# Feed-forward contraction of a hybrid decoder layer: accumulator set-up and the first half's layer norm move from GpSimd and ScalarE to VectorE

## The reference

```python
x = layer_norm(alpha * x + mix, ln1_g, ln1_b)
ff = jnp.square(jax.nn.relu(x @ w_ff1)) @ w_ff2
x = layer_norm(alpha * x + ff, ln2_g, ln2_b)        # alpha = 2 ** 0.25
```

## Time and profile before

| | us |
|---|---|
| median of 3 runs | 2074.1 |
| the three runs | 2073.32, 2074.1, 2076.65 |
| span of the profiled execution | 2073.1 |
| PE busy in it | 2050.5 (99%) |
| DVE, ACT, POOL busy | 1395.7, 993.8, 488.9 |
| bytes moved | 374.34 MB, mean 181 GB/s |

### The profile page before, as it was taken

How to read it: one execution, slowest core, us unless ns; L and a number is a source line. 1 busy time by engine, 2 the same in 40 slices (tenths; PEclk the granted TensorE clock), 3 DMA queues, 4 the chain that set the end, 5 groups by cost and what they waited for, 6 DMA issues and landing times. The chain is left out here.

```text
span 2073.1 us, 28942 instructions
## 1 busy us (share of the span) xinstructions
PE 2050.5 (99%) x11360; PEld 1678.8 (81%) x11360; DVE 1395.7 (67%) x1969; ACT 993.8 (48%) x1339; POOL 488.9 (24%) x537
## 2 busy tenths in 40 slices
PE   9999999999999999999999999999999999999998
PEld 8778788878887888788888888888788888778887
DVE  6687568656856698766657767566485645965477
ACT  5444544454444457655556545455333333633333
POOL 3000000000000013244301344345696600810000
PEclk9999999999999999999999999999999999999999
DMA  6144252425142524466666777868968555666664
GB/s 186 53 121 120 64 170 56 133 61 173 52 123 64 181 72 153 154 211 211 215 214 203 279 259 248 279 244 293 335 206 292 194 195 190 223 225 194 194 220 163
DMA packets 244327, 374.34 MB, mean 181 GB/s; under 512 B 18032, under 2 KB 119504, under 8 KB 244192
## 3 DMA queue, kind: packets, MB, share of 16 engines
q1 hardware_dynamic: 213536, 275.82, 41.2%
q0 software_dynamic: 30656, 96.67, 14.3%
HBM read 272.81 MB, written 99.61 MB: 180 GB/s over the span
## 5 line engine op out<-in xcount | busy, mean ns | idle before, releaser
L1751 DVE TENSOR_TENSOR w_lo<-w_b,w_hi 128x1024 fp32r<-128x1024 f32 x142 | 207.3, 1464 | 202.3 <-ACT w_hi L1718 202.3
L1751 DVE TENSOR_TENSOR w_lo<-raw,w_hi 128x1024 fp32r<-128x1024 f32 x142 | 198.9, 1405 | 119.0 <-ACT w_hi L1718 118.7
L1718 ACT ACTIVATE w_hi<-raw 128x1024 fp32r<-128x1024 f32 x142 | 150.2, 1059 | 217.8 <-PE main L71 86.9
L1718 ACT ACTIVATE w_hi<-w_b 128x1024 fp32r<-128x1024 f32 x142 | 150.0, 1057 | 173.9 <-PE aux L71 73.3
L69 PE MATMUL main<-xT_lo,w_hi 128*128 128x512 f32 x512 | 210.5, 411 | 0.0
L71 PE MATMUL main<-xT_hi,w_hi 128*128 128x512 f32 x512 | 200.1, 391 | 0.0
L70 PE MATMUL main<-xT_hi,w_lo 128*128 128x512 f32 x512 | 199.7, 390 | 0.0
L1130 DVE TENSOR_TENSOR w_lo<-raw,w_hi 128x1024 fp32r<-128x1024 f32 x114 | 138.8, 1222 | 89.1 <-ACT w_hi L805 87.4
L69 PE MATMUL sc<-x_lo,w_hi 128*128 128x512 f32 x448 | 174.4, 389 | 1.8 <-DVE z L2214 1.8
L70 PE MATMUL sc<-x_hi,w_lo 128*128 128x512 f32 x448 | 174.3, 389 | 0.0
L71 PE MATMUL sc<-x_hi,w_hi 128*128 128x512 f32 x448 | 174.3, 389 | 0.0
(11 more groups left out here) (305 smaller groups left out, 4667.7 us busy)
## 6 DMA issues: line engine op xcount, KB each, us to landing
raw<-in_w_in_dram SPq DMA_DIRECT2D x80, 512.0 KB, 3.8
h_dram<-z SPq DMA_DIRECT2D x64, 512.0 KB, 4.3
raw<-h_dram SPq DMA_DIRECT2D x112, 256.0 KB, 2.7
w_b<-h_dram SPq DMA_DIRECT2D x112, 256.0 KB, 2.7
h_dram<-h_s SPq DMA_DIRECT2D x48, 512.0 KB, 3.8
raw<-in_w_out_dram SPq DMA_DIRECT2D x32, 512.0 KB, 3.7
raw<-in_w_ff_dram SPq DMA_DIRECT2D x32, 512.0 KB, 6.4
w_b<-in_w_ff_dram SPq DMA_DIRECT2D x32, 512.0 KB, 4.7
```

Of the source, the lines that this page charges most:

```text
L1718: act.activation(hi, slot_tile(ff, m), ACT.Copy).then_inc(ff.hi_done, 1)
L1751: dve.tensor_tensor(lo, slot_tile(ff, m), hi.bitcast(F32), ALU.subtract).then_inc(ff.lo_done, 1)
```

## The change

Six things change, all in `feed_forward`.

- POOL loads the rows g1 and b1 and all accumulator tiles, and does no arithmetic on them. The scaling of the two rows is gone.
- DVE sets up the accumulators: `residual_scaled` is (acc * alpha) * g1 and `residual_shifted` is b1 * alpha + acc, both on 128x512. They stand around `slot_low` in slots k = 4, 6, 8, 10 of eight products (`INIT_PLACES`).
- The first half's statistics are split: column half 1 of tiles 0 to 7 in (0, 5) and (0, 6), column half 0 and the join at `FIRST_DONE`, which are slots 1, 4, 7, 10 of the last product of half 0 and of the first product of half 1.
- DVE finishes the first half with `centred` and `scaled` in the two slots after each join, as it does the second half's.
- ACT gives rstd only; its 128x1 copy and the 128x1024 normalisation of the first half are gone.
- POOL only stores the first half's tiles, when `out_ready` says so.

```diff
+FIRST_DONE = [(0, 6, 1), (0, 6, 4), (0, 6, 7), (0, 6, 10), (1, 0, 1), (1, 0, 4), (1, 0, 7), (1, 0, 10)]
+INIT_PLACES = [(0, 0), (0, 1), (0, 2), (0, 3), (0, 4), (0, 5), (1, 1), (1, 2)]
...
         load_row(g1_row, ln1_g)
         load_row(b1_row, ln1_b)
-        for c in range(4):
+        for c in range(NT):
             load_acc(0, c, 4 + 2 * c)
-        pool.wait_ge(row_landed, 16 * 2)
-        for row in (g1_row, b1_row):
-            pool.tensor_scalar(row[:, :], row[:, :], ALPHA, None, ALU.mult).then_inc(row_scaled, 1)
...
-        init(0)
         for c in range(NT):
             load_acc(1, c, 2 * KF + 2 * c)
         load_row(g2_row, ln2_g)
         load_row(b2_row, ln2_b)
-        init(1)
-        pool.wait_ge(row_landed, 16 * 4)
         for c in range(NT):
-            finish(c)
+            pool.wait_ge(out_ready, 2 * c + 2)
+            pool.dma_start(out_rows[P * c:P * c + P, :], acc[0][:, c, :]).then_inc(out_stored[c], 16)
...
+        def residual_scaled(hf, i):
+            c, d = INIT_ORDER[i]
+            cols = slice(512 * d, 512 * d + 512)
+            dve.wait_ge(row_landed, 16 * 2)
+            dve.wait_ge(acc_landed[hf][c], 16)
+            dve.scalar_tensor_tensor(out=acc[hf][:, c, cols], in0=acc[hf][:, c, cols], scalar=ALPHA,
+                                     in1=g1_row[:, cols], op0=ALU.mult, op1=ALU.mult).then_inc(init_step, 1)
...
+            init = None
+            if (hf, at) in INIT_PLACES and 4 <= k < 12 and k % 2 == 0:
+                init = divmod(4 * INIT_PLACES.index((hf, at)) + (k - 4) // 2, 16)
+                residual_scaled(*init)
             if s + 4 < 2 * CONTRACT_SLOTS:
                 slot_low(dve, ff, EXPAND_SLOTS + s + 4)
-            if hf == 1 and at == 0 and 2 <= k < 10:
-                statistics(0, k - 2, 28)
+            if init is not None:
+                residual_shifted(*init)
...
+            if (hf, at, k) in FIRST_DONE:
+                c = FIRST_DONE.index((hf, at, k))
+                half_statistics(0, c, 0, 24 if c < 4 else 28)
+                join_statistics(c)
+            elif (hf, at, k - 1) in FIRST_DONE:
+                if (hf, k) == (0, 2):
+                    dve.wait_ge(row_landed, 16 * 4)
+                centred(0, FIRST_DONE.index((hf, at, k - 1)), scale_step)
+            elif (hf, at, k - 2) in FIRST_DONE:
+                c = FIRST_DONE.index((hf, at, k - 2))
+                scaled(0, c, scale_step, c + 1, out_ready)
```

More of the change, by code:

```diff
@@ L2179, in _ @@
                 slot_high(act, ff, EXPAND_SLOTS + s + 4)
-            if hf == 1 and at == 0 and 3 <= k < 11:
-                normalise(0, k - 3)
+            if (hf, at, k) in FIRST_DONE:
+                inverse_deviation(0, FIRST_DONE.index((hf, at, k)))
             if hf == 1 and (at, k) in HEAD:
-                inverse_deviation(HEAD.index((at, k)))
+                inverse_deviation(1, HEAD.index((at, k)))
         for c in range(TAIL, NT):
-            inverse_deviation(c)
+            inverse_deviation(1, c)
     @block.vector
@@ L2203, in join_statistics @@
             dve.tensor_scalar(nmean[:, c:c + 1], mvar[:, c, 0:1], -1.0, None, ALU.mult).then_inc(ln_stats, 1)
[L2205 to L2208, removed]
         def completed(chunk, i, src, tile):
@@ L2298, in _, with centred, scaled, residual_shifted @@
         last_sum(CHUNKS - 1)
-        def centred(c, step):
-            dve.wait_ge(ln_stats, NT + c + 1)
-            dve.scalar_tensor_tensor(out=acc[1][:, c, :], in0=acc[1][:, c, :], scalar=nmean[:, c:c + 1],
+        def centred(hf, c, step):
+            dve.wait_ge(ln_stats, NT * hf + c + 1)
+            dve.scalar_tensor_tensor(out=acc[hf][:, c, :], in0=acc[hf][:, c, :], scalar=nmean[:, c:c + 1],
                                      in1=g2_row[:, :], op0=ALU.add, op1=ALU.mult).then_inc(step, 1)
-        def scaled(c, step, n, ready):
+        def scaled(hf, c, step, n, ready):
             dve.wait_ge(step, n)
-            dve.wait_ge(ln_step, 3 * NT + 2 * c + 2)
+            dve.wait_ge(ln_step, 2 * (NT * hf + c) + 2)
             for d in range(2):
                 cols = slice(512 * d, 512 * d + 512)
-                dve.scalar_tensor_tensor(out=acc[1][:, c, cols], in0=acc[1][:, c, cols], scalar=rstd[:, c:c + 1],
+                dve.scalar_tensor_tensor(out=acc[hf][:, c, cols], in0=acc[hf][:, c, cols], scalar=rstd[:, c:c + 1],
                                          in1=b2_row[:, cols], op0=ALU.mult, op1=ALU.add).then_inc(ready, 1)
+        def residual_scaled(hf, i):
[5 more added lines that the diff above has]
+                                     in1=g1_row[:, cols], op0=ALU.mult, op1=ALU.mult).then_inc(init_step, 1)
+        def residual_shifted(hf, i):
+            c, d = INIT_ORDER[i]
+            cols = slice(512 * d, 512 * d + 512)
+            dve.wait_ge(init_step, 16 * hf + i + 1)
+            dve.scalar_tensor_tensor(out=acc[hf][:, c, cols], in0=b1_row[:, cols], scalar=ALPHA,
+                                     in1=acc[hf][:, c, cols], op0=ALU.mult, op1=ALU.add).then_inc(init_done, 1)
         for s in range(2 * CONTRACT_SLOTS):
```

58 lines of the change are left out of this document (15 added, 43 removed).

## The result

| kernel | median | from..to | runs | ratio to before, same chip |
|---|---|---|---|---|
| before | 2073.16 | 2071.53..2078.55 | 17 | |
| changed | 2077.83 | 2074.88..2081.09 | 17 | 1.0018 [1.0012, 1.0025] |
| before, second set | 2073.17 | | 22 | |
| changed, second set | 2075.86 | 2072.03..2080.44 | 11 | 1.0015 [1.0006, 1.0023] |

(Times in us; a ratio is that of the undisturbed runs, its 95% interval in brackets.) The changed kernel is 3.8 us slower, 2.5 to 5.2 by the interval. That is under the 0.2% (4.1 us) that the prediction called no change, and it repeats with the same sign. The forecast was +1.9 and 2076.0, with the range 2071.0 to 2082.0. It was added to a median of 2074.1 from three runs; the 17 runs put that median at 2073.16.

A forecast was written before the change was run, and what follows sets the result against it. PE was taken to bound the kernel, busy 2050.5 of 2073.1 us. 2073.1 - 12.0 (old losses) + 12.2 (slot 8 late) + 1.7 (clock) = 2075.0; +1.9 on the median of 2074.1 gave 2076.0, range 2071.0 to 2082.0.

The forecast's parts named there:

- What PE loses before, 12.0: PE's lost time in the contraction before the change, around 1490, 1504 and 1810: 12.0 us, all the change could give back.
- POOL's arithmetic goes, gain 6.85: Contraction near 1504 and 1810: DVE's low parts fall to 1.2, stalls of 5.77 and 1.08 us go, gain 6.85.
- DVE's set-up, priced at 0: 64 set-up operations on 32 slots: DVE runs up to 1.5 us late, under a cover of 5.8; cost 0.
- The finish on DVE, priced at 0: First half's finish, four tiles: DVE falls 4.3 us behind with the adds, under the cover of 5.8; cost 0.
- Rival 3: Finish of the first half: DVE becomes the bound, PE loses 1 to 3 us, 2077 to 2079; chance 0.05.
- The first set-up operation, 12.2 late: After slot 7: DVE waits for rows and tile 0, landing at 1476.2, so slot 8 starts 12.2 us late.
- The clock, 1.7: Behind the idle before slot 8: PE's clock falls, costing 1.7 us, twice that at most.
- The tile for slot 10, priced at 0: Slot 10's iteration: tile 3 lands by 1492.6, ready at 1494.7, before slot 14 at 1496.2; cost 0.
- The 5.11 of the old start goes: Slots 0 to 17: 5.11 us returned, as slot 16's operand is loaded after the rows and tiles are through.
- The sum: Whole kernel: 2073.1 - 12.0 + 12.2 + 1.7 = 2075.0, so +1.9 us, giving 2076.0 on the median.
- rival 1: Before slot 8: tile 0 lands at 1480.8, slot 8 16.8 us late, total 2080.6 to 2082.3; chance 0.27.
- rival 2: Before slot 8: short stall, tile 0 landed before 1473, total 2071 or below; chance 0.12.

The follow-up runs named there:

- e3: Kernel before with only the accumulator set-up moved to DVE, first half still finished by POOL and ACT: 2082.38 us, ratio 1.0046.
- e4: Changed kernel with set-up and row scaling back on POOL, first half's finish still on DVE: 2068.54 us, ratio 0.9975.
- e2: Changed kernel with the first product's four set-ups in slots 12 to 15 in place of 4, 6, 8, 10: 2067.14 us, ratio 0.9969.
- e11: Changed kernel unaltered, its fourth profile: own time of the profiled execution 2077.99 us.
- e9: Changed kernel with the first product's four set-ups in slots 8, 10, 12, 14: 2071.03 us, ratio 0.9979.
- e1: Changed kernel unaltered, its second profile: 2075.86 us, ratio 1.0015.
- e10: Changed kernel unaltered, its third profile: own time of the profiled execution 2077.21 us.
- e12: Kernel before unaltered, its second profile: own time of the profiled execution 2070.75 us.
- e5: Changed kernel with POOL loading the two rows and tiles 0 and 1 ahead of its last w_ff2 round: 2071.92 us, ratio 0.9994.
- e6: e2 with POOL loading the two rows and tiles 0 and 1 ahead of its last w_ff2 round: 2070.42 us, ratio 0.9985.
- e8: e4 with POOL loading the two rows and tiles 0 and 1 ahead of its last w_ff2 round: 2070.09 us, ratio 0.9983.

## Why the prediction was right

By its own steps:

- **What PE loses before, 12.0.** In the same profile the ledger has 12.2. The kernel before loses 11.15 in another profile, so 12.0 was a little more than typical. This hardly changes the difference.
- **POOL's arithmetic goes, gain 6.85.** Right. The changed kernel has no idle PE between 1790 and 1830 and no late slot at 1504, since the hole is its only wait. e3 against e4 shows whose it is: with POOL's finish it stays (8.91 of 10), without it is gone (10.00), though POOL does its set-up in e4.
- **DVE's set-up, priced at 0.** Right for the changed kernel: 64 operations of 0.685 and, the first one's load apart, not one wait of PE behind them. Packed more densely, in e2, they share in one wait of 0.52.
- **The finish on DVE, priced at 0.** Right, with its working: the period is 8.60 as forecast from HEAD, and PE never waits in it. Rival 3 falls.
- **The first set-up operation, 12.2 late.** The mechanism is right in each link: DVE idle behind a load (16.33; I had said some 18), PE idle from slot 7's end, slot 8 at 1476.88 (1478.2). It measured 11.15. The difference is where POOL stood: it issued the row 23.25 after slot 0, in place of 24.33 in the profile of before. Behind that issue the forecast had 7.6 to landing and the trace 7.78 to DVE's start. The landing was an estimate from rows in which SP was loading too, so that it came out so near is in part luck: the same kernel took 9.0 in e11. In the other three profiles the hole was 12.84, 11.50 and 11.21.

The DMA part has a rival figure in the Trainium skill, "DMA: Bandwidth & Descriptors", section "Anatomy of one DMA — SWDGE (gpsimd) path": 2.0 us plus the bytes at 436 GB/s. The page gives this for one transfer; taking rows and tile as one of 1.57 MB, my estimate by it is 5.6 after the first issue, and a hole 2 shorter. The trace disagrees: 7.7 to 7.8 in three profiles, 9.0 to 11.8 in e11, e3 and e9. Here the measurement decides.

- **The clock, 1.7.** This term was somewhat small. It was taken from a stop of 2.53. The four profiles of the changed kernel lost 2.3, 2.3 (e1), 1.8 (e10) and 1.9 (e11). All are inside the bound that the prediction gave (twice 1.7).
- **The tile for slot 10, priced at 0.** Right: DVE did wait for it, 3.24 at 1490.49, and PE did not.

```profile
1490.49 0.69 DVE L2272 SCALAR_TENSOR_TENSOR acc<-acc,g_row 128x512 f32<-128x512 f32 x1 [3.24 <-DMA acc<-normed_dram]
```

- **The 5.11 of the old start goes.** Right in the changed kernel: slot 16 starts at 1500.99, forecast 1501.7, with no other wait ahead of it. The likely reason is that the hole lets the transfers run without SP: DMA share 1.0 while nobody computes. In e4, without the hole, the start's cost was there again (3.11 and the clock).
- **The sum.** +1.9 against +3.8 [2.5, 5.2]. In the pair of profiles hole and clock were 13.5 where the forecast had 13.9: two errors of opposite sign, -1.05 and +0.6, which is luck. Over all profiles the changed kernel loses 14.6, not 13.9 (a hole of 11.7 on average, 0.5 less than forecast; the clock 2.1, 0.4 more; 0.8 of other waits, for which the forecast had no term), and the kernel before 11.7, not 12.0. That makes +2.9. The last 0.9 lies within the interval of the timed runs, and I can't assign it. Some profiles (e1, e3 to e9, e11, e12) have a further wait of 0.7 to 1.2 between 2041 and 2055, in the last eight slots; e12 is the kernel before, so it is not the change's alone.
- **The rivals.** A longer stall (rival 1) wanted a landing at about 1478.5 or later; the four landings were at 1475.0 to 1477.5. e1, whose landing was the latest of the four, shows that it was near. The short stall (rival 2) needed POOL at its rows 5 sooner; e3 had it 5.8 sooner after slot 0 and still a hole of 9.3, as its loads took longer; e5 did it on purpose and still did not reach it, for its own reason.

## What to carry to other kernels

When arithmetic moves to an engine that works in a fixed order, look at the first instruction that waits for a transfer: everything behind it waits too. Taking it up four or eight slots later, one line of the order, turned +0.18% into -0.21% and -0.31%. Before moving such a load earlier instead, ask what it pushes aside: here it was the operand of the slot that was to be saved.

## What the runs showed of the hardware that I had not expected

- **What a hole costs in clock.** In the five profiles with a hole of 9 to 13, PE stood for 2.1 (changed), 3.8 (e1), 3.9 (e3), 4.8 (e11) and 4.9 (e10) before PEclk fell. Behind the hole it lost 2.3, 2.3, 2.4, 1.9 and 1.8 at half clock. Behind waits of 2.7 to 6.2 it lost 1.5 to 1.8 (before, e4, e5, e6, e8, e9). So the loss doesn't follow the length of the stop: 11.5 of it cost 1.8 in e10, 9.3 cost 2.4 in e3. In e10 the clock comes back sooner after the restart (1478.38) than in the changed kernel's first profile. Its stretches:

```profile
1481.00:1482.00 1.00, 1.00 (x4) 0.71 (x4) 1.00 (x2) 0.00 (x0) 0.00 (x0) 0.50 0.40 145
1482.00:1483.00 1.00, 1.00 (x6) 0.83 (x5) 1.00 (x2) 0.00 (x0) 0.00 (x0) 0.92 0.94 340
```

  PE idle for 1.0 at most (e2, e12) left the clock at 1.00.
- **Row loads are slow for their bytes.** At a DMA share of 1.00 the stretch at 1471, while the two rows were under way, moved 213 GB/s, and the one at 1475, with tiles, 414. A row is one 4 KB line spread over 128 partitions, a tile is 128 lines. At these rates, by my estimate, the two rows took about twice the engines' time of two tiles. The windows of POOL's queue (packets, MB, share), at 1470:1472 and at 1474:1476:

```profile
q0 software_dynamic: 127, 0.45, 104.8%
...
q0 software_dynamic: 234, 0.83, 101.3%
```

- **A small load among large ones.** SP's 256 KB took 16.3 to land beside a burst of rows, tiles and w_ff2 loads from POOL's queue (e5), nearly the 16.0 of the earlier trace rows. At both places where the burst was put the delay went with it.
